# V and the projection strips in two halves of the tokens, every strip group by seven block products

## The chip, the cores and the metric

The kernel runs on one core of a Trainium2 chip. The metric is device time in microseconds of one execution, here the median of several runs.

## The reference, cut to what matters

Float32 inputs: x is 2048 x 1024, the combined projection `w_in` is 1024 x 5120.

```python
h = rms_norm(x, norm_g)
proj = einsum('bsd,de->bse', h, w_in)          # 2048 x 1024 by 1024 x 5120
u_pool, z_pool, q, k, v, z_attn, gate_logits = split(proj)
y_pool = multiscale_pool(u_pool, pool_w, pool_scale) * silu(z_pool)
attn = stick_breaking_attention(q, k, v)       # causal, 8 heads of 64
y_attn = attn * silu(z_attn)
gates = sigmoid(gate_logits + b_gate)
merged = gates[0] * (y_pool @ w_pool_up) + gates[1] * (y_attn @ w_attn_up)
x = x + merged @ w_out
return rms_norm(x, final_g)
```

`multiscale_pool` takes, for four groups of 128 channels of u, the trailing mean over 2, 4, 8 and 16 positions minus the value itself, then a 128 x 128 map and a scale per channel.

## The kernel before, in words

**Three matmuls for one.** Every float32 operand of a product is split into a high part (a copy to the type fp32r, by ScalarE) and a low part (the difference, by VectorE or GpSimd). `split3` (L73) makes one product of three matmuls: high by high, high by low, low by high. A product of 128 x 128 weights with 512 tokens is the unit; a strip is 128 columns of `w_in`, and one strip for one chunk of 512 tokens is 8 k-tiles, so 24 matmuls (`strip_product`, L85).

**Seven block products.** Two strips by two chunks of tokens, cut in halves of k, are a product of 2 x 2 blocks. By a Winograd scheme it takes seven block products (parts) of 4 k-tiles, 12 matmuls each, instead of eight. It needs forms of the weights (S1 to S4, four 128x512 operations) and of h (T1 to T4), and the parts' results are added up in sums (`take`, `add_part`, `join`). Names: A11, A12, A22, S1 to S4 are weight operands; B11, B21, B22, T1 to T4 are their partners made of h. The sizes of blocks: a form of h in `hT` has 4 k-tiles by 512 tokens, high and low.

**The four stages**, each a block of programs for all engines with a barrier behind it:

- `stage1` (L307): for each of 16 tiles of 128 tokens, the RMS statistics (ScalarE squares, VectorE `mean` L486, `factors` L493 with the diagonal at L504), TensorE spreads the factor over partitions (`spread`, L539), VectorE scales the transposed x (`scale` L472, at L481, 8 operations), ScalarE makes the high part (L435), GpSimd the low part (L401), and TensorE makes V for the tile, 24 matmuls (L551, L559, L567). VectorE copies V out (L470). TensorE goes through the tiles in the order of the tokens. V's weights (`wv_hi`, `wv_lo`) are split once. At its end TensorE makes the first plain unit of the first strip.
- `stage2` (L610): 12 strips (u in four groups, then the eight of q and k) and part of the z_pool strips, all by plain units: 49 units of 24 matmuls, in the order of the list `units`. High parts of a strip's weights by ScalarE (L794), low ones by GpSimd (L887). The four groups of u go through the pooling on VectorE (L999 levels, L1009, the cast L1016, L1018) over all 2048 tokens, and TensorE maps the result (`mix`, L1045). Late in this stage VectorE makes T1 to T4 from high and low parts of h (`first_forms` L947, `last_forms` L964), for tokens of both halves: those of chunks 2 and 3 go to the scratch `form_scratch` in HBM, those of chunks 0 and 1 in place at the end (L983). For the last strips and z_pool it runs through the chunks in the order 2, 3, 0, 1.
- `stage3` (L1111): attention for four pairs of heads, 320 items, and between them a filler of the rest of the strips (z_pool, z_attn, gates). The filler is a generator (`projections`, L1526) that the item loop advances by a table: each item has a cost, and `due` (L1208) says how many filler matmuls are done after it. Group 0 is four plain parts, of which one is made in stage 2; groups 1 to 23 are seven parts each. All other engines follow the same table (`PART_END`, `W_STEP`, `RESULT`). Weights of a part go through a ring of five slots: ScalarE's high (L1600), then GpSimd's low (`step` in `low_w`, L1770), as soon as the part five before is done.
- `stage4` (L1867): the gated merge, the output projection (by seven parts too) and the last norm.

**Order.** Every engine runs its program in order and waits on semaphores. All loads and stores are issued by SyncE (SP) in one queue. GpSimd's operations in stage 3 each wait for the one before.

## Time and profile before

| what | value |
|---|---|
| median of 3 runs | 1587.72 us (1587.53 to 1587.85) |
| span of the profiled execution | 1586.6 us |
| TensorE matmuls | 1556.0 us busy, 98% of the span, 7926 |
| VectorE | 1236.3 us, 78% |
| ScalarE | 772.7 us, 49% |
| GpSimd | 1004.9 us, 63% |
| mean granted clock of TensorE | 0.997 |
| DMA | 245.79 MB, mean 155 GB/s |

The profile is one execution, taken by the hardware profiler; its own time is known as its span, from the first to the last instruction, and the median of the runs is 1.1 us above it. PE is TensorE, PEld its weight loads, DVE VectorE, ACT ScalarE, POOL GpSimd, SP SyncE. Busy time of PE is the union of matmuls that overlap in the array, so the duration of one matmul is more than the distance to the next.

### The profile page before, as it was taken

The numbers are of one execution on the slowest core, as the hardware profiler recorded it, in microseconds if no ns is written. First come the engines' busy times: TensorE is split into PE (matmuls) and PEld (weight loads), VectorE is DVE, ScalarE is ACT, GpSimd is POOL, SyncE is SP. The second block draws the span as 40 slices with busy tenths as digits, with TensorE's granted clock in tenths as the row PEclk, the third lists the DMA queues.
The fourth block names the chain that finished last, engine by engine and source line by source line (L and its number), as shares of the span: only waits on it lengthen the run. The fifth ranks groups of instructions, "written<-read, shape, count | busy, mean of one in ns | idle before, by whom it ended". The sixth has DMA issues, their size and how long they took to land. (4 is left out here: it accounts for less than half of the span.)

```text
span 1586.6 us, 24736 instructions
## 1 busy us (share of the span) xinstructions
PE 1556.0 (98%) x7926; PEld 1299.3 (82%) x7926; DVE 1236.3 (78%) x1658; ACT 772.7 (49%) x1490; POOL 1004.9 (63%) x707
## 2 busy tenths in 40 slices
PE   7999999999999999999998999999999999999998
PEld 6888888888888888888877888888788788888886
DVE  6745424784888889998898988889888756677987
ACT  4422222214666666666665666666666512233342
POOL 4531102431788888888877887889986534456774
PEclk9999999999999999999999999999999999999999
DMA  7633335665434243343595443333422687864552
GB/s 246 231 129 145 133 108 184 241 182 161 128 116 113 79 119 104 108 136 91 174 317 182 121 129 87 111 106 110 119 78 65 206 280 252 262 196 161 184 189 110
DMA packets 164225, 245.79 MB, mean 155 GB/s; under 512 B 47729, under 2 KB 81009, under 8 KB 164098
## 3 DMA queue, kind: packets, MB, share of 16 engines
q1 hardware_dynamic: 164098, 244.20, 49.4%
q8 instruction: 67, 1.10, 0.3%
q14 instruction: 60, 0.49, 0.1%
HBM read 158.15 MB, written 85.99 MB: 154 GB/s over the span
## 5 line engine op out<-in xcount | busy, mean ns | idle before, releaser
L1697 DVE TENSOR_TENSOR_SCAN left<-keep,left 128x512 f32<-128x512 f32 x192 | 301.6, 1571 | 39.9 <-issue 23.4
L1770 POOL TENSOR_TENSOR ring<-raw,ring 128x512 fp32r<-128x512 f32 x138 | 240.1, 1740 | 71.8 <-ACT ring L1600 56.6
L1517 PE MATMUL psum<-hT,ring 128*128 128x512 f32 x644 | 264.1, 410 | 4.9 <-DMA hT<-form_scratch 3.6
L1521 PE MATMUL psum<-hT,ring 128*128 128x512 f32 x644 | 262.5, 408 | 0.0
L1519 PE MATMUL psum<-hT,ring 128*128 128x512 f32 x644 | 261.8, 407 | 0.0
L1606 ACT ACTIVATE keep<-psum 128x512 f32<-128x512 f32 (+3 forms) x320 | 170.9, 534 | 139.8 <-PE psum L1543 131.6
L1613 ACT ACTIVATE wt<-psum 128x512 fp32r<-128x512 f32 (+3 forms) x320 | 170.8, 534 | 104.8 <-PE psum L1551 102.0
L1703 DVE TENSOR_TENSOR wt<-psum,wt 128x512 fp32r<-128x512 f32 (+3 forms) x320 | 189.6, 593 | 11.6 <-ACT wt L1613 8.5
L1563 PEld LDWEIGHTS psum<-wt,vm 128*128 128x128 f32 x1088 | 170.9, 188 | 26.6 <-issue 1.5
L1563 PE MATMUL psum<-wt,vm 128*128 128x256 f32 x1088 | 181.3, 281 | 0.4 <-DVE row_sum L1712 0.4
L1551 PE MATMUL psum<-ident,left 128*128 128x128 f32 x1088 | 170.9, 272 | 2.5 <-DVE wt L1703 2.3
L1551 PEld LDWEIGHTS psum<-ident,left 128*128 128x128 f32 x1088 | 136.2, 140 | 44.5 <-issue 6.6
L1694 DVE TENSOR_TENSOR_SCAN left<-keep,floor 128x512 f32<-128x512 f32 (+3 forms) x128 | 143.6, 1122 | 20.2 <-ACT keep L1606 18.2
L75 PE MATMUL psum<-hT,w_parts 128*128 128x512 f32 x392 | 152.6, 389 | 0.5 <-POOLq L899 0.5
L77 PE MATMUL psum<-hT,w_parts 128*128 128x512 f32 x392 | 152.5, 389 | 0.0
L76 PE MATMUL psum<-hT,w_parts 128*128 128x512 f32 x392 | 152.5, 389 | 0.0
L1517 PEld LDWEIGHTS psum<-hT,ring 128*128 128x128 f32 x644 | 121.6, 189 | 26.5 <-issue 4.2
L1521 PEld LDWEIGHTS psum<-hT,ring 128*128 128x128 f32 x644 | 121.6, 189 | 17.9
L1519 PEld LDWEIGHTS psum<-hT,ring 128*128 128x128 f32 x644 | 121.6, 189 | 17.1
L887 POOL TENSOR_TENSOR w_parts<-w_raw,w_parts 128x1024 fp32r<-128x1024 f32 x13 | 34.5, 2654 | 149.0 <-ACT w_parts L794 149.0
L1770 POOL TENSOR_TENSOR y_out<-row_sum 64x128 f32<-64x128 f32 x128 | 110.5, 863 | 26.0 <-DVE row_sum L1712 8.5
L1542 PE MATMUL psum<-km,qm 128*128 128x512 f32 (+3 forms) x320 | 115.9, 362 | 3.6 <-DMA qm<-qk_scratch 1.8
(232 smaller groups left out, 3338.7 us busy)
## 6 DMA issues: line engine op xcount, KB each, us to landing
raw<-in_w_strips SPq DMA_DIRECT2D x92, 256.0 KB, 4.0
qm<-qk_scratch SPq DMA_DIRECT2D x128, 128.0 KB, 4.1
gate<-gate_scratch SPq DMA_DIRECT2D x64, 256.0 KB, 4.5
hT<-form_scratch SPq DMA_DIRECT2D x28, 512.0 KB, 8.6
xt<-in_x SPq DMA_DIRECT2D x16, 512.0 KB, 5.0
xT<-in_x_T SPq DMA_DIRECT2D x16, 512.0 KB, 3.9
qk_scratch<-staging SPq DMA_DIRECT2D x32, 256.0 KB, 2.8
qk_scratch<-store_lo SPq DMA_DIRECT2D x32, 256.0 KB, 3.5
```

The lines of the kernel that those rows point to most:

```text
L75: pe.matmul(out, w_hi, m_hi, start=start, stop=False)
L76: pe.matmul(out, w_hi, m_lo, start=False, stop=False)
L1517: pe.matmul(o, hi, m_hi, start=k == 0, stop=False)
L1519: pe.matmul(o, hi, m_lo, start=False, stop=False)
L1521: last = pe.matmul(o, lo, m_hi, start=False, stop=k == HK - 1)
L1551: last = pe.transpose(bank_t(n)[:, j * P:(j + 1) * P], left[:, n % LN, a:a + P], ident[:, :])
L1563: last = pe.matmul(bank_o(row), vm[:, t % VN, j, :], wt[:, n % WN, j, :, :].rearrange("p a q -> p (a q)"), start=first and j == 0, stop=fi ...
L1606: act.activation(keep[:, n % 2, CH - w:CH], bank_s(n)[:, 0:w], ACT.Sigmoid, scale=-SCALE).then_inc(keep_done, 1)
L1613: act.activation(wt[:, n % WN, 0:w // P, 0, :], bank_t(n)[:, 0:w].rearrange("p (j q) -> p j q", q=P), ACT.Copy).then_inc(wt_hi_done, 1)
L1697: dve.tensor_tensor_scan(left[:, n % LN, span][:, ::-1], k, k, carry, ALU.mult, ALU.bypass).then_inc(scanned, 1)
L1703: dve.tensor_tensor(wt[:, n % WN, 0:w // P, 1, :], bank_t(n)[:, 0:w].rearrange("p (j q) -> p j q", q=P), wt[:, n % WN, 0:w // P, 0, :].bit ...
L1770: pool.tensor_tensor(out_, a, b, op).then_inc(s, 1)
```

## The change

`stage1` and `stage2` are replaced by one block, `front`. The tokens are taken in two halves of 1024. For each half it makes V for eight tiles and then six groups of seven parts (two of u, four of q and k); a slot of its schedule is one V tile or one part. The order is 8 tiles, 42 parts, 8 tiles, 42 parts, 2 parts of stage 3's group 0.

- Tiles of a half alternate between its two chunks, so that after every second tile T1 to T4 can be made for 128 columns. They are made during V, from the scaled fp32 tiles (`xT`, scaled in place) as far as these are there: six VectorE operations per pair of tiles (`first_forms`, `last_form`), four high parts on ScalarE (`form_high`), and low parts on VectorE (`form_lows`) but for those in `LATE_T`, which GpSimd makes (T3 in the first half, T3 and T4 in the second).
- The copy of V out of PSUM moves from VectorE to ScalarE and has one buffer. The statistics of tiles 8 to 15 are made between parts of the first half (`STAT_PARTS`). V's weights are loaded and split a second time (`RELOAD`), since the pooling uses their place.
- The strips' weights go through the ring of five in the front too, and each strip is loaded once per half. A strip group has five additions (`add_part`) and two joins on VectorE, two copies of PSUM (`take`) on ScalarE; for q and k also four high copies (`result_high`) on ScalarE and four low parts (`result_low`) on VectorE.
- Pooling works on 1024 tokens at a time, in steps between the parts, with the last 16 columns kept (`tail`); the four mixes of a half come after its parts 12, 16, 20 and 24.
- All seven forms of the first half are stored to the scratch during the first 28 parts. Stage 3 then begins with the second half of the tokens.
- In stage 3 group 0 is made of seven parts like the others; the first two of them are made in the front. The filler goes from 2004 matmuls to 1992.

The diff, cut to its core:

```diff
-def strip_product(pe, out, w_hi, w_lo, hT, c):
...
-        stage1(nc, sem, psum, Arena(nc, free_at, end), ident, ident_r, gcol, bcol, pscol,
...
-        stage2(nc, sem, psum, Arena(nc, free_at, end), Arena(nc, free_at, heads.at), Arena(nc, heads.at, end), ident, v_d,
...
+        front(nc, sem, psum, at, free_at, hT_at, ident, ident_r, gcol, bcol, pscol, v_ends, hT, ring, raws, staging,
+              x, x_T, norm_gT, w_v, b_gateT, pool_scaleT, w_strips, pool_w, pool_fix, v_d, qk_d, mix_d, form_d, head_loads)
...
+FRONT_GROUPS, FRONT_TILES = 12, TT // 2
+HALF_GROUPS = FRONT_GROUPS // 2
+HALF_PARTS = HALF_GROUPS * FORMS
+READY_PARTS = 2
+def tile_slot(n):
+    return n if n < FRONT_TILES else n + HALF_PARTS
+def part_slot(r):
+    return r + FRONT_TILES if r < HALF_PARTS else r + 2 * FRONT_TILES
...
+    LATE_T = {0: (T3,), 1: (T3, T4)}
+    T_ORDER = (T3, T1, T2, T4)
...
+    MIX_AFTER = (12, 16, 20, 24)
+    STAT_PARTS = {n: 14 + 2 * (n - FRONT_TILES) for n in range(FRONT_TILES, TT)}
+    RELOAD = 28
```

On GpSimd:

```diff
+            def tile_step(n):
+                tile_low(n)
+                if n % FRONT_TILES >= 2:
+                    if n % 2 == 0:
+                        form_low(n - 1, T3)
+                    elif T4 in LATE_T[n // FRONT_TILES]:
+                        form_low(n - 2, T4)
...
+            for s in range(SLOTS):
+                n = step_at(s)
+                if n is not None:
+                    tile_step(n)
...
+                if s == 5:
+                    pool.wait_ge(pw_hi_done, 1)
+                    step(pw_lo[:, :, :], pw[:, :, :], pw_hi[:, :, :].bitcast(F32), ALU.subtract, pw_lo_done, 1)
+                for w in splits_at(s):
+                    low_w(w)
```

On VectorE:

```diff
+            def first_forms(n):
...
+                dve.tensor_tensor(raw_t(n, T3), scaled(n, 1), scaled(n, 0), ALU.subtract).then_inc(t_raw, 1)
+                dve.tensor_tensor(raw_t(n, T1), scaled(n, 0), tile_of(n - 1, 0, 0).bitcast(F32),
+                                  ALU.subtract).then_inc(t_raw, 1)
+                dve.wait_ge(t_raw, RAW_OPS * pair + 2)
+                dve.tensor_tensor(raw_t(n, T1), raw_t(n, T1), tile_of(n - 1, 0, 1).bitcast(F32),
+                                  ALU.subtract).then_inc(t_raw, 1)
+                dve.wait_ge(t_raw, RAW_OPS * pair + RAW_OF[T1])
+                dve.tensor_tensor(raw_t(n, T2), scaled(n, 1), raw_t(n, T1), ALU.subtract).then_inc(t_raw, 1)
...
+            def tile_step(n):
+                i = n % FRONT_TILES
+                first = n < FRONT_TILES
+                if first and i + 1 < FRONT_TILES:
+                    mean(n + 1)
+                scale(n)
+                if i + 1 < FRONT_TILES:
+                    if first:
+                        factors(n + 1)
+                    make_diag(n + 1)
+                if i % 2 == 1:
+                    if i >= 3:
+                        form_lows(n - 2)
+                    first_forms(n)
+                elif i >= 2:
+                    last_form(n - 1)
```

On TensorE:

```diff
+            def make_part(r):
+                g, j = divmod(r, FORMS)
+                if r >= 4:
+                    g0, j0 = divmod(r - 4, FORMS)
+                    if j0 in (A11, S1):
+                        pe.wait_ge(taken, 2 * g0 + (1 if j0 == A11 else 2))
+                    else:
+                        pe.wait_ge(summed, 5 * g0 + ADD_OF[j0])
+                pe.wait_ge(w_lo_done, r + 1)
...
+            for s in range(2, SLOTS):
+                if s in TILE_AT:
+                    project_v(TILE_AT[s])
+                else:
+                    r = PART_AT[s]
+                    make_part(r)
```

`closing_at` gives, in the slot of the last tile of a half, the forms that are left: VectorE's `last_form` and `form_lows`, GpSimd's T3 (and T4). `splits_at` gives ring low 0 in slot 5, 1 and 2 in slot 6, 3 and 4 in slot 7, and then ring low r + 5 in the slot after part r. `low_w` has, for a group's first operand, S3 and S2 ahead of the ring low and S1 behind it, and S4 behind the second's.

## Rows read from the trace of the kernel before

**Rows 1.** Busy time by stretch: count in brackets, then granted clock, DMA share, GB/s.

```profile
0.00:109.00 109.00, 101.06 (x438) 81.52 (x439) 70.06 (x226) 46.84 (x87) 51.16 (x43) 0.98 0.64 215
109.00:389.00 280.00, 279.20 (x1229) 229.44 (x1228) 149.12 (x155) 71.57 (x113) 67.36 (x47) 1.00 0.50 164
```

**Rows 2.** TensorE's waits from 0 to 410 us, the longest in total.

```profile
PE psum L539 <- DVE spare L504: 2.9, 3, 1.3
```

**Rows 3.** TensorE's timeline at the boundary of stages 1 and 2: start, duration.

```profile
109.04 0.39 PE L75 MATMUL psum<-hT,w_parts 128*128 128x512 f32 x1
...
114.26 0.39 PE L77 MATMUL psum<-hT,w_parts 128*128 128x512 f32 x1
115.16 0.47 PE L75 MATMUL psum<-hT,w_parts 128*128 128x512 f32 x1 [0.51 <-POOLq L899]
```

**Rows 4.** TensorE's timeline in the V stage, two spreads in a row.

```profile
64.52 0.38 PE L539 MATMUL psum<-spare 128*128 128x128 f32 x2
...
70.23 0.38 PE L539 MATMUL psum<-spare 128*128 128x128 f32 x2
```

**Rows 5.** VectorE's timeline in the V stage, tile 2 and a later one.

```profile
24.04 2.16 DVE L481 SCALAR_TENSOR_TENSOR scaled<-xT,gcol,psum 128x128 f32<-128x128 f32 x8 [1.32 <-PE psum L539]
...
65.00 2.16 DVE L481 SCALAR_TENSOR_TENSOR scaled<-xT,gcol,psum 128x128 f32<-128x128 f32 x8 [1.21 <-PE psum L539]
67.07 0.68 DVE L470 COPY staging<-psum 128x512 f32<-128x512 f32 x1
67.67 0.14 DVE L488 TENSOR_SCALAR stat<-stat 128x1 f32<-128x1 f32 x1
...
68.28 0.27 DVE L496 TENSOR_SCALAR stat<-stat 128x1 f32<-128x1 f32 x1 [0.27 <-ACT stat L424]
...
68.78 0.71 DVE L504 TENSOR_SCALAR spare<-ident,stat 128x128 f32<-128x128 f32 x1
```

**Rows 6.** Timeline of the same tile, ScalarE's first high part and GpSimd's two low parts.

```profile
66.15 0.63 ACT L435 ACTIVATE hT<-scaled 128x512 fp32r<-128x512 f32 x1 [2.39 <-DVE scaled L481]
...
66.86 2.54 POOL L401 TENSOR_TENSOR hT<-scaled,hT 128x512 fp32r<-128x512 f32 x2 [0.80 <-ACT hT L435]
```

**Rows 7.** Timeline of forms of h in the strip stage, VectorE and GpSimd.

```profile
299.87 0.68 DVE L956 TENSOR_TENSOR t_raw<-hT 128x512 f32<-128x512 f32 x1
300.47 0.68 DVE L958 TENSOR_TENSOR t_raw<-hT 128x512 f32<-128x512 f32 x1
...
306.36 0.69 DVE L975 TENSOR_TENSOR t_raw<-hT,t_raw 128x512 f32<-128x512 f32 x1
...
307.07 1.28 POOL L893 TENSOR_TENSOR t_parts<-t_raw,t_parts 128x512 fp32r<-128x512 f32 x1 [2.02 <-ACT t_parts L831]
...
307.08 1.81 DVE L977 TENSOR_TENSOR t_raw<-t_raw,hT 128x512 f32<-128x512 f32 x1
```

**Rows 8.** Timeline in stage 4, two VectorE operations on SBUF and one of GpSimd.

```profile
1407.53 2.39 DVE L2359 TENSOR_TENSOR form_t<-late,form_t 128x512 fp32r<-128x512 f32 x2
...
1407.69 1.67 POOL L2511 TENSOR_TENSOR rows<-rows,gate 128x512 f32<-128x512 f32 x1 [3.87 <-DVE gate L2331]
```

**Rows 9.** Groups of VectorE, 109 to 389 us, pooling: busy us, mean ns.

```profile
L999 DVE TENSOR_TENSOR sums<-u 128x2048 f32<-128x2048 f32 x4 | 9.2, 2293 | 53.3 <-ACT u L809 53.3
...
L1016 DVE CAST pl_hi<-pooled 128x2048 fp32r<-128x2048 f32 x4 | 4.9, 1224 | 0.1
```

**Rows 10.** GpSimd's ring lows (ns, min/median/max), and the busy time of stage 4's parts.

```profile
L1770 POOL TENSOR_TENSOR ring<-raw,ring x138: 1274/1757/3603, 409.1 to 1229.8; 128x512 fp32r<-128x512 f32 x138
...
1459.00:1478.00 19.00, 19.00 (x84) 15.63 (x85) 17.26 (x30) 6.91 (x15) 12.57 (x8) 1.00 0.54 193
```

**Rows 11.** Busy time around tile 2, granted clock third from the end, and TensorE's timeline there.

```profile
24.00:28.00 4.00, 2.95 (x12) 1.80 (x10) 3.58 (x14) 2.17 (x4) 2.09 (x2) 1.00 0.32 96
28.00:32.00 4.00, 3.49 (x10) 2.84 (x10) 3.12 (x10) 1.39 (x4) 1.17 (x2) 0.58 0.99 341
...
28.94 2.05 PE L559 MATMUL psum<-wv_lo,hT 128*128 128x512 f32 x4
```

**Rows 12.** SP's timeline in the strip stage, four form stores.

```profile
160.50 3.60 SPq L728 DMA_DIRECT2D form_scratch<-hT  x4
```

More of the change, by code:

```diff
@@ new lines, in make_diag, with scale @@
+            def make_diag(n):
+                dve.wait_ge(statistics, 4 * n + 4)
+                if n >= 2:
+                    dve.wait_ge(spread_done, n - 1)
+                dve.tensor_scalar(diag[:, n % 2, :], ident[:, :], stat[:, n, 3:4], stat[:, n, 5:6],
+                                  ALU.mult, ALU.mult).then_inc(diag_done, 1)
+            def scale(n):
+                dve.wait_ge(xT_in[n % 3], DMA * (n // 3 + 1))
+                dve.wait_ge(spread_done, n + 1)
+                for k in range(KT):
+                    tile = xT[:, n % 3, k, :]
+                    last = dve.scalar_tensor_tensor(tile, tile, gcol[:, k:k + 1], spread_bank(n), ALU.mult, ALU.mult)
+                    if k % HK == HK - 1:
+                        last.then_inc(scaled_done, 1)
@@ L531, in _ @@
+            assert nexts == [None, None]
         @block.tensor
         def _(pe):
-            def spread(t):
-                pe.wait_ge(diag_done, t + 1)
-                if t >= 2:
-                    pe.wait_ge(scaled_done, 2 * (t - 1))
-                pe.matmul(psum[:, t % 2, 0:P], ones[:, :], diag[:, t % 2, :], start=True,
-                          stop=True).then_inc(spread_done, 1)
-            def part_of(t, k, part):
-                return tile_of(t, k // HK, part)[:, k % HK, :]
@@ L545, in high_high, with spread, part_of @@
-            def high_high(t, ks):
+            def spread(n):
+                pe.wait_ge(diag_done, n + 1)
+                if n >= 2:
+                    pe.wait_ge(scaled_done, 2 * (n - 1))
+                pe.matmul(spread_bank(n), ones[:, :], diag[:, n % 2, :], start=True, stop=True).then_inc(spread_done, 1)
+            def part_of(n, k, part):
+                return tile_of(n, k // HK, part)[:, k % HK, :]
+            def high_high(n, ks):
+                f, i = divmod(n, FRONT_TILES)
@@ new lines, in mix @@
+            def mix(f, q):
+                win = POOL_ORDER[q]
+                pe.wait_ge(pool_lo, 4 * f + q + 1)
+                if f == 0 and q == 0:
+                    pe.wait_ge(pw_lo_done, 1)
+                for c in range(2):
+                    tok = slice(c * CH, (c + 1) * CH)
+                    if q == 0:
+                        pe.wait_ge(v_copied, FRONT_TILES * (f + 1))
+                    else:
+                        pe.wait_ge(mix_out, mix_use(f, q - 1, c) + 1)
+                    split3(pe, v_bank(c), pw_hi[:, win, :], pw_lo[:, win, :], pl_hi[:, tok], pl_lo[:, tok],
+                           True, True).then_inc(mixed, 1)
@@ L1843, in _ @@
             for s in range(-9, END):
-                for g in range(1, GROUPS):
+                for g in range(GROUPS):
                     for j in (S1, S3):
```

1519 lines of the change are left out of this document (774 added, 745 removed).

## The prediction

> **What bounds the kernel now.** I read the busy time by stage first: in the V stage (0 to 109 us) TensorE is busy 101 of 109 us, in the strip stage (109 to 389) 279.2 of 280 [rows 1]. TensorE's own waits come next: the largest sum in the first 410 us is 2.9 us, for the diagonal that `spread` reads [rows 2]. So the front is TensorE issuing matmuls at its own pace. A strip product's matmuls start 5.22 us apart over 23 steps, 0.227 us each [rows 3]; the 389 ns "mean of one" overlaps the next matmul and would overstate a matmul by 1.7 times. A V tile's cycle is 5.71 us, from one `spread` to the next [rows 4].
>
> **What is removed.** Before: 49 plain strip units of 24 matmuls in the strip stage and its first unit in stage 1, plus 3 plain parts in stage 3; of these 48 units belong to the twelve u, q, k strips and 4 to z_p's first group. Thirteen groups of four units (96 matmuls) become seven parts of 12 (84). That is 13 x 12 = 156 matmuls fewer; V (384), the mixes (48) and stage 4 keep theirs. 156 x 0.227 = **-35.4 us**, all on the path. One stage boundary goes: the next matmul after 114.26 came at 115.16 instead of 114.49 [rows 3], -0.7. Together -36.1, if TensorE stays the bound.
>
> **What VectorE gets in V.** Now a tile costs VectorE: scale 2.07 us (from 65.00 to 67.07), means 0.33, factors 0.50, diag 0.28, taken as free of GpSimd [rows 5]; the V copy moves to ScalarE. New per pair of tiles in the first half: six tensor_tensor to make T1 to T4 and three low parts, all with two SBUF operands. Such operations start 0.60 us apart, 0.72 when one waits for the one before [rows 7]. Per pair: 2 x 3.18 + 9 x 0.60 + 3 x 0.13 = 12.2 us, against 2 x 5.71 = 11.42 for TensorE. Already over.
>
> Worse is GpSimd. A VectorE operation on two SBUF tiles that is issued at 307.08 beside a GpSimd one (307.07, 1.28 us) takes 1.81 instead of 0.68: it starts when the other has ended [rows 7]. And of two such VectorE operations in a row with GpSimd waiting, GpSimd gets in between: 1.67 us instead of 1.28, and the two take 2.39 [rows 8]. So they take turns: 1.28 held by GpSimd, 0.54 by VectorE. The diag does so too: 0.71 us at 68.78, ending just as GpSimd's low parts do (66.86 + 2.54) [rows 5, 6].
>
> Laid along one tile with the scale's start at 0: ScalarE's first high part 1.15 [rows 5, 6], GpSimd's lows 1.86 to 3.14 and 3.25 to 4.5, with diag between them; VectorE's next form waits until 4.5. An odd tile then has three lows and four forms: 1 + 6 more at 0.60, gaps 0.4, mean 0.33, period 9.4. An even one has two forms with GpSimd's T3 low between them: 4.5, 5.1, 6.4, 6.9, mean, period 7.3. A pair is 16.7 us, not 11.42.
>
> First half: VectorE is free at 22.7 before scale(2), which starts at 24.0 [rows 5]; four forms of tile 1 (2.4 + 0.4) and a mean (0.33) put it at 25.8. Scale(7) comes 7.3 + 9.4 + 7.3 + 9.4 + 7.3 = 40.7 later, at 66.5, and V(7) starts 1.8 after it, at 68.3. Now V ends at 109.0 [rows 3], so V(7) starts at 57.6 and ends at 109.0 - 8 x 5.71 = 63.3. Before `tile_low(7)` GpSimd's order has pw_lo, S3, S2, the first ring low and S1: five operations, 6.4 us, with VectorE's lows and T3 in turn another 2; so V(7)'s low operand is there at 76, and V(7) ends near 79.5, 16.2 later than now. T2's low part is behind a closing sequence of VectorE and GpSimd in turn, 2.6 us late for part 2. Sum **+19**. Bounds: 3, if VectorE never waits (12.2 a pair); 25, if it waits in full for all five GpSimd operations of each of three pairs (12.2 + 6.4 = 18.6).
>
> Second half: statistics are made earlier, three low operations become two, and GpSimd has T3 and T4. The same laying out gives 9.6 and 7.0; from scale(9) (8.3, no lows yet, but a ring low) to scale(15) 8.3 + 7.0 + 9.6 + 7.0 + 9.6 + 7.0 = 48.5. Scale(9) starts 1.5 after V(8), so V(15) ends 1.5 + 48.5 + 1.8 + 5.5 = 57.3 after V(8) starts, not 8 x 5.71 - 0.15 = 45.5, and T2's low is 1.7 late: **+13.5**; bounds 0 (VectorE alone: 2 x 2.35 + 8 x 0.60 + 0.4 = 9.9 a pair, under 11.42) and 18 (9.9 + 6 x 1.28 = 17.6 a pair).
>
> **The strips.** A group is 84 x 0.227 = 19.05 us of TensorE, 114.3 for a half's six, and mixes add 24 x 0.227 = 5.4. GpSimd has 7 ring lows and 4 forms a group, 11 x 1.28 = 14.1 (its unhindered minimum, 1.27 [rows 10]), no joins. VectorE holds the shared turn for 2 joins and, for q and k, 4 lows: 3.3. Together 17.4 of 19.05. Stage 4 does the same seven parts with 8 GpSimd operations, 7 lows and two 128x1024 finishes, 10.2 + 3.8 + 2.1 = 16.1, and TensorE is busy 19.00 of 19.00 us there [rows 10]. So a q or k group is covered. Pooling isn't: per half ten levels, four pooled and four pl_lo at half of 2.29 less overhead, 1.08, and four casts at 0.55, about 22 us [rows 9], in parts 6 to 21. There the turns want 25 x 1.28 + 22.4 + 5 = 59.6 us where TensorE offers 16 x 2.72 + 4.1 = 47.6. That is 12 us late, taken up partly by the ring (five splits ahead) and the four banks. With the ring just filled and GpSimd late in the first half: **+8**; second half, ring full: **+5**. Bounds 0 (all absorbed) and 13 each. The second loading of V's weights (2 MB), its four lows (1.2 each [rows 9], in the lock sum 4.3) and 6 MB more of strips lie beside parts; before, DMA ran at half share there [rows 1], cost nothing if it lands some parts early, which parts 28 to 40 give it.
>
> **The clock.** With V bound by VectorE, TensorE idles some 2.6 of 8.3 us. From 24 to 28 it was busy 2.95 of 4 us, and from 28 to 32 the granted clock was 0.58, a stretch at 1.2 GHz between stretches at 2.4; the four matmuls from 28.94 took 2.05 instead of 1.07 [rows 11]. That drop cost about 1.6 us (eight matmuls in 3.4 us, not 1.8). In most tiles such a drop fits in the idle time; the ends of V(7) and V(15) don't have it. **+3**, bounds 0 and 13 x 1.6 = 21.
>
> The Trainium skill (TensorE: Matmul & The Clock Gate, "Why this matters for your kernels") puts a fall of the clock down to an idle gap between bursts of matmuls, a whole one, not to a partly busy stretch. By that rule this term would be 0 and the sum 1597; the rows show the fall after a stretch 74% busy. The same page (Back-to-back issue gap) gives 131 ns a matmul of 512 columns in a real stream; by it 156 matmuls would be an estimated 20.4 us, and the sum 1615. The trace has 227.
>
> **Sum.** -36.1 + 19 + 13.5 + 8 + 5 + 3 = +12.4 on the profiled span of 1586.6. The median of the runs shown is 1587.7, 1.1 above that span; I add it: **1600 us**.
>
> Edits at nothing: SP issues per strip group 4 loads, up to 8 stores of results and 7 of forms; at the 0.90 us of a form store, the longest here [rows 12], 19 issues take 17 of 19.05 us, and the first wait in its order is for results of two parts before, so nobody waits for it while it keeps up; the 80 VectorE operations that make the forms in the strip stage now hide under TensorE, and their removal gives nothing; V's stores share one buffer, but have a tile's 5.7 us or more each; the key, query and value loads before stage 3 still have some twelve parts (33 us); stage 3 starts with group 0 as parts, and there TensorE's filler is spread over 1187 - 389 us as before.
>
> **Rivals.** (a) *TensorE bounds everything*: 1587.7 - 36.1 = 1551.6. For it: copies and statistics were moved off VectorE; against it, 12.2 us already exceeds 11.42 with no contention. 0.08. (b) *The other side: only V pays.* The turns shared by GpSimd and VectorE bind in V, but in the strips the ring and banks absorb pooling, and the clock holds: V costs 24 to 32, so 1587.7 - 36.1 + 28 = 1580. It decides at a total loss of 36: below, the change is faster. Against it: 59.6 us of turns in 47.6. 0.26. (c) *My forecast*, 1600, its own range 1588 to 1609: 0.46. (d) *The turns bind the strips through and through*: ScalarE's result copy waits for VectorE's sum and stands ahead of the next split, so a late VectorE makes GpSimd late with no slack to use; 13 in each half, and V's tiles at the half clock add 6 more: 1600 + 13 + 6 = 1619. 0.20.
>
> **The numbers.** 1600; the range takes in (b) and most of (d): 1564 to 1620; (a) and the tail of (d) stay out. A measurement of this kernel can tell 0.2%, 3.2 us. Faster: (a), (b) but its upper edge, a sliver of (c): 0.35. Same: edges of (b) and (c): 0.08. Slower: 0.57.
>
> **What would show it.** Right: in the new V stages TensorE's starts of tiles lie 7 to 9.5 us apart, alternating; its waits name ScalarE's or GpSimd's parts of h, VectorE is busy over 90%; form operations of 1.8 us beside GpSimd ones; TensorE waits for ring lows in parts 8 to 24 and hardly later; the granted clock in V is under 0.9. Wrong: V tiles at 5.7 us; no wait of TensorE on the ring; GpSimd operations at 1.3 throughout; a matmul spacing other than 0.227; or a wait on the reload of V's weights, the one transfer that I cost at nothing.

## The result and the profile after

| what | before | after |
|---|---|---|
| median of 4 runs each | 1587.62 us | 1657.62 us (1654.57 to 1660.69) |
| ratio | | 1.0443, 95% interval 1.0422 to 1.0464 |
| span of the profiled execution | 1586.6 us | 1658.9 us |
| TensorE matmuls | 1556.0 us busy, 7926 | 1552.7 us busy, 7770 |
| VectorE | 1236.3 us | 1354.2 us |
| GpSimd | 1004.9 us | 1188.5 us |
| mean granted clock | 0.997 | 0.979 |

The change is 70 us slower, where 12 were forecast and 1620 was the upper end. The 156 matmuls are gone; all of the loss is waiting and half clock. First the busy time by stretch, cut at the starts of the first matmul of V, of the first strips, of the second V, of the second strips, and at the end of the front; columns as in [rows 1] (busy us of PE, PEld, DVE, ACT and POOL, each with its count).

```profile
0.00:79.60 79.60, 61.52 (x230) 46.89 (x231) 64.16 (x139) 38.70 (x71) 45.95 (x37) 0.91 0.52 182
79.60:227.20 147.60, 127.59 (x532) 101.19 (x530) 108.84 (x139) 58.34 (x108) 104.09 (x66) 0.95 0.80 261
227.20:290.70 63.50, 52.62 (x206) 41.69 (x207) 58.33 (x98) 22.58 (x40) 41.44 (x28) 0.89 0.28 89
290.70:431.90 141.20, 130.80 (x557) 106.53 (x555) 102.16 (x98) 45.11 (x80) 105.45 (x67) 0.96 0.49 135
```

Where [rows 1] had TensorE busy 279.2 of 280 us in the strips, it now has 127.6 of 147.6 and 130.8 of 141.2. The granted clock is under 1 in every stretch. TensorE's waits from 0 to 450 us (total, times, longest), against 2.9 us in [rows 2]:

```profile
PE psum L1167 <- ACT staging L797: 19.5, 6, 4.7
PE psum L75 <- ACT staging L848: 15.7, 3, 6.4
PE psum L1655 <- ACT sum_a L1767: 7.0, 1, 7.0
PE psum L75 <- DVE staging L1016: 5.0, 1, 5.0
PE psum L75 <- POOL ring L680: 3.3, 3, 1.7
```

The two largest name ScalarE, the least busy engine: its copy of V (L797) and its scale of a mix (L848), both into the one buffer `v_out`. Neither is slow itself (0.6 us); each stands behind other work. The first, at tile 2 of V, from the timelines of DVE, ACT, PE:

```profile
29.89 1.64 DVE L964 TENSOR_TENSOR raw_forms<-raw_forms,hT 128x512 f32<-128x512 f32 x1
33.56 2.16 DVE L935 SCALAR_TENSOR_TENSOR xT<-xT,gcol,psum 128x128 f32<-128x128 f32 x8 [1.24 <-PE psum L1155]
28.24 0.63 ACT L787 ACTIVATE hT<-xT 128x512 fp32r<-128x512 f32 x1 [0.41 <-DVE xT L935]
28.77 1.65 ACT L791 ACTIVATE hT<-raw_forms 128x512 fp32r<-128x512 f32 x3
30.33 0.58 ACT L797 ACTIVATE staging<-psum 128x512 f32<-128x512 f32 x1
30.96 2.07 PE L1167 MATMUL psum<-wv_hi,hT 128*128 128x512 f32 x4 [4.71 <-ACT staging L797]
```

V(0) has long been done, but its copy comes after tile 2's high parts and three of the forms. TensorE starts 4.71 us late and at the half clock (four matmuls in 2.07 us), its `spread` comes late, and VectorE waits 1.24 us for that: the lateness goes round. A mix's scale, from the timelines around mix 2 of the first half:

```profile
144.88 2.15 DVE L1056 TENSOR_TENSOR level<-u 128x1024 f32<-128x1024 f32 x1
148.05 0.69 DVE L1026 TENSOR_TENSOR front_sum_c<-front_sum_d,front_sum_c 128x512 f32<-128x512 f32 x1
148.77 0.63 ACT L831 ACTIVATE front_store<-front_sum_c 128x512 fp32r<-128x512 f32 x1 [5.14 <-DVE front_sum_c L1026]
149.83 0.67 ACT L848 ACTIVATE staging<-psum,pscol 128x512 f32<-128x512 f32 x1
150.55 0.79 PE L75 MATMUL psum<-pl_hi,pw_hi 128*128 128x512 f32 x1 [6.40 <-ACT staging L848]
```

Pooling holds VectorE, the join comes late, ScalarE's result copy waits 5.14 us for it, the scale of the mix before stands behind that copy, and TensorE waits 6.40 us with its parts behind the mix. Before part 79 it is a transfer:

```profile
398.21 2.40 SPq L564 DMA_DIRECT2D raw<-in_w_strips  x4
408.33 0.43 DVE L123 TENSOR_TENSOR v_raw<-v_prev,v_raw 128x256 f32<-128x256 f32 x1 [10.40 <-DMA v_prev<-v_scratch]
409.46 0.68 DVE L1016 TENSOR_TENSOR staging<-psum,staging 128x512 f32<-128x512 f32 x1
410.20 0.80 PE L75 MATMUL psum<-hT,ring 128*128 128x512 f32 x1 [4.97 <-DVE staging L1016]
```

The value load was issued behind four loads of strips, VectorE waited 10.40 us for it, and additions queued behind. And in the closing of the first V the turns are as forecast:

```profile
72.71 1.53 POOL L680 TENSOR_TENSOR b<-xT,b 128x512 fp32r<-128x512 f32 x1
74.39 1.54 POOL L680 TENSOR_TENSOR hT<-xT,hT 128x512 fp32r<-128x512 f32 x1
73.04 1.75 DVE L947 TENSOR_TENSOR raw_forms<-xT,hT 128x512 f32<-128x512 f32 x1
74.82 1.66 DVE L950 TENSOR_TENSOR raw_forms<-raw_forms,hT 128x512 f32<-128x512 f32 x1
```

**Stage 3.** Its first filler matmul starts 7.4 us after the last of the front (the wait L1655 above). The last store of the front is issued at 434.3, and SyncE issues the next block's first load at 438.4: the front ends only when its last results have landed. The boundary before took 0.84 us. Then its items themselves are slower: from the first score to the last 863.1 us, 847.2 before. One place, 30 us after the start:

```profile
465.69 1.53 POOL L1901 TENSOR_TENSOR sum_c<-sum_d,sum_c 128x512 f32<-128x512 f32 x1
467.26 0.63 ACT L1781 ACTIVATE staging<-sum_c 128x512 f32<-128x512 f32 x1 [3.85 <-POOL sum_c L1901]
467.92 1.26 DVE L1868 TENSOR_TENSOR sum_c<-sum_c,staging 128x512 f32<-128x512 f32 x1 [1.82 <-ACT staging L1781]
469.10 0.68 DVE L1834 TENSOR_TENSOR wt<-psum,wt 128x512 fp32r<-128x512 f32 x1
469.93 0.62 PE L1686 MATMUL psum<-ident,left 128*128 128x128 f32 x3 [3.36 <-DVE wt L1834]
```

**Where the 72.3 us of the span come from.** The front, had TensorE bounded it, would have brought stage 3's first matmul from 389.6 to 356 us (144 matmuls and one boundary less); it came at 439.1. The 83 between are: first V +16, first strips +28 (147.6 against 42 x 12 + 24 matmuls at 0.227, which are 119.8), second V +18 (63.5 against 8 x 5.71), second strips +16 (140.9 against 44 x 12 + 24 matmuls, 125.3), the end of the front +7, and -2 since the old strip stage was not quite at 0.227 either. After it: 12 matmuls fewer -2.7, items and their start some +20, the rest (last score to last matmul) +5. With the 33.5 that the front saved, 83 - 33.5 - 2.7 + 20 + 5 = 72.

### The profile page after: what moved, and what is told of

It reads as the page before. It is cut to its first block and busy times, and to the rows that moved or that the text cites. A ratio compares the mean times of both kernels' runs of the same rounds, so it can differ in the third digit from the quotient of the medians.

```text
span 1658.9 us, 25189 instructions
## 1 busy us (share of the span) xinstructions
PE 1552.7 (94%) x7770; PEld 1285.2 (77%) x7770; DVE 1354.2 (82%) x1753; ACT 824.9 (50%) x1597; POOL 1188.5 (72%) x818
## 5 line engine op out<-in xcount | busy, mean ns | idle before, releaser
L1901 POOL TENSOR_TENSOR ring<-raw,ring 128x512 fp32r<-128x512 f32 x140 | 236.7, 1690 | 80.9 <-ACT ring L1735 65.7
L1655 PE MATMUL psum<-hT,ring 128*128 128x512 f32 x664 | 273.3, 412 | 12.2 <-ACT sum_a L1767 7.0
L1659 PE MATMUL psum<-hT,ring 128*128 128x512 f32 x664 | 271.2, 408 | 0.0
L1657 PE MATMUL psum<-hT,ring 128*128 128x512 f32 x664 | 270.8, 408 | 0.0
L1834 DVE TENSOR_TENSOR wt<-psum,wt 128x512 fp32r<-128x512 f32 (+3 forms) x320 | 189.5, 592 | 12.4 <-ACT wt L1748 9.5
L1686 PE MATMUL psum<-ident,left 128*128 128x128 f32 x1088 | 171.3, 272 | 11.3 <-DVE wt L1834 11.1
L680 POOL TENSOR_TENSOR ring<-raw,ring 128x512 fp32r<-128x512 f32 x76 | 119.9, 1578 | 72.0 <-ACT ring L841 64.3
L1825 DVE TENSOR_TENSOR_SCAN left<-keep,floor 128x512 f32<-128x512 f32 (+3 forms) x128 | 139.2, 1088 | 20.1 <-ACT keep L1741 18.1
L1655 PEld LDWEIGHTS psum<-hT,ring 128*128 128x128 f32 x664 | 126.0, 190 | 34.3 <-ACT sum_a L1767 7.8
L75 PE MATMUL psum<-hT,ring 128*128 128x512 f32 x344 | 137.6, 400 | 11.9 <-DVE staging L1016 5.0
L1659 PEld LDWEIGHTS psum<-hT,ring 128*128 128x128 f32 x664 | 126.0, 190 | 18.5
L1657 PEld LDWEIGHTS psum<-hT,ring 128*128 128x128 f32 x664 | 126.2, 190 | 17.5
L76 PE MATMUL psum<-hT,ring 128*128 128x512 f32 x344 | 136.2, 396 | 0.0
L77 PE MATMUL psum<-hT,ring 128*128 128x512 f32 x344 | 136.1, 396 | 0.0
```

The lines of the kernel that those rows point to most:

```text
L75: pe.matmul(out, w_hi, m_hi, start=start, stop=False)
L76: pe.matmul(out, w_hi, m_lo, start=False, stop=False)
L77: return pe.matmul(out, w_lo, m_hi, start=False, stop=stop)
L1655: pe.matmul(o, hi, m_hi, start=k == 0, stop=False)
L1657: pe.matmul(o, hi, m_lo, start=False, stop=False)
L1659: last = pe.matmul(o, lo, m_hi, start=False, stop=k == HK - 1)
```

## The experiments

The table has the medians, the ratio to the kernel before on the same chip, and, from each one's trace, the start of V(7)'s last matmul and the lengths (starts of first matmuls) of first strips, second V, second strips, the way from the front's last matmul to stage 3's first, and the items (first score to last).

| run | us | ratio (95%) | V(7) | strips 1 | V 2 | strips 2 | gap | items |
|---|---|---|---|---|---|---|---|---|
| changed | 1657.6 | 1.0443 (1.0422-1.0464) | 79.4 | 147.6 | 63.5 | 140.9 | 7.4 | 863.1 |
| e1 copy first | 1651.8 | 1.0404 (1.0384-1.0423) | 79.5 | 148.8 | 56.0 | 138.4 | 7.8 | 862.8 |
| e2 statistics late | 1656.8 | 1.0437 (1.0416-1.0458) | 77.7 | 147.5 | 61.3 | 141.4 | 8.4 | 864.7 |
| e3 values | 1661.0 | 1.0470 (1.0444-1.0496) | 79.9 | 147.6 | 61.3 | 135.1 | 11.4 | 861.7 |
| e4 no forms | 1643.6 | 1.0349 (1.0328-1.0370) | 75.9 | 147.7 | 51.5 | 139.9 | 8.1 | 863.7 |
| e5 low 7 first | 1656.0 | 1.0413 (1.0384-1.0443) | 71.7 | 155.4 | 57.7 | 140.2 | 8.5 | 865.1 |
| e6 pooling small | 1645.6 | 1.0358 (1.0341-1.0374) | 76.9 | 140.7 | 61.2 | 131.0 | 9.1 | 867.6 |
| e7 small stores | 1649.3 | 1.0394 (1.0373-1.0416) | 79.1 | 145.6 | 62.6 | 138.1 | 7.4 | 857.9 |
| e8 GpSimd small | 1630.4 | 1.0268 (1.0253-1.0283) | 76.0 | 139.1 | 59.2 | 130.8 | 6.3 | 861.2 |
| e9 phase | 1646.7 | 1.0364 (1.0337-1.0390) | 77.7 | 151.6 | 60.7 | 140.7 | 8.2 | 852.5 |
| e10 orders | 1627.1 | 1.0234 (1.0207-1.0260) | 79.6 | 141.9 | 55.9 | 132.1 | 8.6 | 853.7 |
| e11 bare | 1599.2 | 1.0062 (1.0038-1.0086) | 67.7 | 134.7 | 46.0 | 131.6 | 4.4 | 857.3 |
| e12 bare and orders | 1568.4 | 0.9876 (0.9844-0.9908) | 67.2 | 124.9 | 47.9 | 125.6 | 3.2 | 844.6 |
| e13 warm | 1658.6 | 1.0440 (1.0403-1.0476) | 77.9 | 147.8 | 60.2 | 139.6 | 8.1 | 862.1 |

The columns are of one profiled execution each, the medians of all runs. Where kernels have the same code, a column shows how far two executions lie apart: V(7) 76.9 to 79.9 and the second V 60.7 to 63.5 (changed, e2, e3, e6, e7, e9), first strips 147.6 to 151.6 (changed, e3, e9), items 861.2 to 867.6 (changed, e1 to e6, e8, e13). Differences below 4 us in one column, 7 in that of the items, show nothing by themselves.

### e1: ScalarE's copy of V first

```diff
             def tile_step(n):
...
+                if n % FRONT_TILES >= 2:
+                    copy_v(n - 2)
                 tile_high(n)
...
-                    copy_v(n - 2)
```

> ScalarE's copy of V out of PSUM is moved in its own order: ahead of the tile's high parts and of the forms' high parts, instead of behind them. Theory 1 (order: TensorE waits in V for a copy that stands behind other work on ScalarE, six times, 19.5 us in all, and VectorE then waits for a late spread): the six waits named after the copy go, even tiles start 2 to 3 us earlier, the clock holds there, and the kernel gets 10 to 20 us shorter than the changed one (1638 to 1648). Theory 2 (the prediction's: VectorE and GpSimd take turns and bind the V tiles): the waits only change their name, to VectorE's scale, and the time stays within 4 us of 1657.6.

1651.8 us, 5.8 less: between the two. The waits for the copy are gone; TensorE's largest in V are now these:

```profile
PE psum L1168 <- ACT hT L787: 8.5, 4, 2.6
PE psum L1187 <- POOL b L680: 6.4, 1, 6.4
```

The second V is 7.5 us shorter (63.5 to 56.0), the first ends where it did, since V(7) now starts earlier and waits 6.4 us for GpSimd's low part instead. So the order cost about 6 us in the second V: of the 19.5 us of waits that named ScalarE's copy, 5.8 came back. VectorE and GpSimd hold the rest.

### e2: statistics' loads later

```diff
-                        if r == first - 4:
+                        if r == first - 1:
                             load_xt(m)
```

> The loads for the statistics of tiles 8 to 15 are issued three parts later in SyncE's order, where the wait for the tile before (a square on ScalarE) is already met. Theory 1 (order: SyncE waits there for ScalarE's square, ScalarE waits for the stores that stand behind it on SyncE, and the scale of a mix stands behind those): the waits of the mixes 2 and 3 in the first half (6.4 and 4.6 us) shrink below 1.5 us each, the two falls of the clock behind them go, and the kernel is 8 to 14 us shorter (1643 to 1650). Theory 2 (pooling on VectorE is late because of the turns): the waits stay, within 3 us of 1657.6.

1656.8 us, first strips 147.5: no effect. The longest wait for a mix's scale is still 5.9 us. That theory of the mixes fell; their chain goes through VectorE (above), not through the stores.

### e3: value tiles

```diff
-    V_PARTS = [HALF_PARTS + i for i in (29, 31, 33, 35)]
+    V_PARTS = [HALF_PARTS + i for i in (26, 30, 34, 38)]
...
-                    if r == first + 1:
+                    if r == first + 2:
                         head_loads.value_diff(dve, u)
```

> The first four value tiles for the attention are loaded at parts 26, 30, 34, 38 of the second half instead of 29, 31, 33, 35, and VectorE works on each one part later after its load than before. Theory 1 (VectorE waits up to 10.4 us for such a load, issued behind four loads of strips, with TensorE's additions behind it): the wait of 5.0 us before part 79 goes with the half clock behind it, 5 to 8 us shorter (1650 to 1653). Theory 2 (turns): TensorE waits there for another addition or ring low instead, within 3 us of 1657.6.

1661.0 us. The wait before part 79 went, and the second strips are 5.8 us shorter; the gap behind the front grew from 7.4 to 11.4 us, and the median is no better. What was gained was paid at the next wait, the end of the block. (The profiled execution took 1655.3 us, 5.7 under the median of its runs.)

### e4: no forms in V

```diff
-                dve.tensor_tensor(raw_t(n, T3), scaled(n, 1), scaled(n, 0), ALU.subtract).then_inc(t_raw, 1)
+                dve.tensor_tensor(raw_t(n, T3)[:, :, 0:4], some, some, ALU.add).then_inc(t_raw, 1)
...
+                act.activation(low_t(n, j), source, ACT.Copy)
+                act.activation(high_t(n, j), source, ACT.Copy).then_inc(t_hi, 1)
```

> As the first of these four, and the making of T1 to T4 in V is left out (VectorE's and GpSimd's operations for them shrink to 4 of 128 columns, ScalarE writes copies of an h tile in their place, one activation more each): the sums of the front are not those of the reference. Theory 2 (turns bind V): V's tiles go at 5.7 to 6.3 us, V(7) ends near 65 and the second V takes 47 us, 25 to 33 us less than the changed kernel, nearly all of it beyond what the first of these runs gives. Theory 1 (order alone): the first run has already given most of it, and this one is less than 8 us under it.

14.0 us under the changed kernel, 8.2 under e1. (All forms and their lows are cut like the first line shown.) The second V falls to 51.5 (45.7 at TensorE's pace); the first gains 3.6 at most, for it still waits for GpSimd's ring work ahead of tile 7's low parts. Beyond e1 the forms are worth 3.6 and 4.5 us in the two V, at the edge of what a column tells: a part of V's price, not most of it. The 8.2 us under e1 are just over the bound of theory 1 and far from what theory 2 asked.

### e5: tile 7's low parts ahead of the ring

```diff
-            return {5: (0,), 6: (1, 2), 7: (3, 4)}.get(s, ())
+            return {6: (0, 1), 7: (2, 3, 4)}.get(s, ())
...
-                if s == 5:
+                if s == 6:
                     pool.wait_ge(pw_hi_done, 1)
```

(with e1's edit)

> As the run with ScalarE's copy of V first, and GpSimd's (and ScalarE's) work on pool_w and on the first three slots' strip weights is moved one slot back, behind the low parts of tile 7. The theory that V(7) waits 6.4 us for GpSimd's order alone: V(7) ends near 75 instead of 79.5, and the kernel takes 4 to 5 us less than that run (1647). Rival: the same five operations then hold the ring's first lows or T3's low for parts 0 to 2, and the time comes out within 2 us of that run.

V(7) ends at 71.7, 7.8 us sooner than in e1, and the first strips take 155.4 instead of 148.8; 1656.0 us, 4.2 above e1, and the intervals of the two ratios overlap. The first part now waits 3.3 us for a ring low of GpSimd's, one of the five operations, and part 2 3.7 us for a form's low part of VectorE's; between 0 and 200 us these are

```profile
PE psum L75 <- POOL ring L680: 3.9, 2, 3.3
PE psum L75 <- DVE hT L974: 3.7, 1, 3.7
```

The strips end no sooner than in e1 (230.9 against 228.5 us): V's end and the strips' start are one budget of GpSimd and VectorE, and this order within it gives nothing.

### e6: most of the pooling left out

```diff
-                        dve.tensor_tensor(to[:, a:W], src[:, a:W], src[:, a - (1 << i):W - (1 << i)],
+                        dve.tensor_tensor(to[:, a:PAD + 64], src[:, a:PAD + 64], src[:, a - (1 << i):PAD + 64 - (1 << i)],
```

> The changed kernel with the pooling left out but for 32 to 80 of its 1024 columns (levels and pooled; its high and low parts are copies of u, the low one a single-operand copy), so the mix scratch is not the reference's. Theory A (pooling makes VectorE late, with GpSimd in turn, and everything behind it: ScalarE's result copies, the scale of a mix, the ring): the strips of the first half take 126 to 132 us instead of 147.6, those of the second 128 to 132 instead of 141, some 25 us less in all (1632). Theory B (the DMA engines, at a share of 0.84 to 1.05 from 143 to 227 us, land results and form stores late): the first half loses only what lies before 143 us, 3 to 8 us, and the kernel 5 to 12.

12.0 us less: 7 in the first strips, 10 in the second; the items, whose code is the same, took 4.5 more in this execution. Half of what theory A asked, and at the upper end of theory B's, which e7 takes up; the first strips are still 21 us above 119.8.

### e7: a quarter of the form stores

```diff
-                sp.dma_start(form_d[j, kk], hT[:, HOME[j], kk, :, :].bitcast(F32)).then_inc(form_stored, DMA)
+                sp.dma_start(form_d[j, kk][:, :, 0:P], hT[:, HOME[j], kk, :, 0:P].bitcast(F32)).then_inc(form_stored, DMA)
```

> The changed kernel with a quarter of each form stored and loaded back (128 of 512 columns, 28 transfers of 128 KB instead of 512 KB each way), so stage 3's second half works on other numbers. Theory B (DMA): the waits after 143 us in the first half (mix 3's 4.6 us, ring lows of parts 31 to 37, the end) go, 8 to 14 us less (1645 to 1650). Theory A (VectorE and GpSimd): within 3 us of 1657.6, since the waits come through additions and ring lows that wait for no transfer.

(The load back is cut in the same way.) 8.3 us less, as theory B had it, but not where it had it: the first strips lose 2 us only, within the scatter, and 5.2 us lie in the items, where the forms are loaded back, 3.3 below the lowest of the same code. Where the rest of the 8.3 lies is open. The DMA engines, busy at a share of 0.80 in the first strips, are not what holds them.

### e8: GpSimd's strip work left out

```diff
-                step(ring[:, w % RING, 1, :, :], at_g[j][:, :, :], ring[:, w % RING, 0, :, :].bitcast(F32),
+                step(ring[:, w % RING, 1, :, 0:4], at_g[j][:, :, 0:4], ring[:, w % RING, 0, :, 0:4].bitcast(F32),
...
+                act.activation(ring[:, w % RING, 1, :, :], source, ACT.Copy)
```

> The changed kernel with GpSimd's work on strip weights in the front left out: S1 to S4 and the low parts on 4 of 128 columns, and ScalarE writes high and low slot as copies of one block (one activation more per part), so V is right and the strips are not. Theory A: without turns VectorE's operations in the strips take 0.6 to 0.7 and 1.2 us instead of 1.3 to 1.8 and 2.2, pooling comes in time, and the strips take 122 to 130 us in the first half and 126 to 132 in the second, 25 to 35 us less in all (1623 to 1633). Theory B: the late stores stay, less than 10 us.

(S1 to S4 are cut in the same way.) 27.2 us less, the most of any single edit; of the 32.0 between the two profiled executions 8.5 are in the first strips, 10 in the second, 3.4 and 4.3 in the two V, where GpSimd's strip work at V's end is left out too. VectorE's operations on the pooled columns, of e8 (count, ns min/median/max), and then of the changed kernel:

```profile
L1079 DVE CAST pl_hi<-level x4: 684/686/710, 101.9 to 144.5; 128x1024 fp32r<-128x1024 f32 x4
L1083 DVE TENSOR_TENSOR pl_lo<-level,pl_hi x4: 1224/1225/1225, 102.6 to 145.2; 128x1024 fp32r<-128x1024 f32 x4
```

```profile
L1076 DVE CAST pl_hi<-level x4: 680/1174/1785, 109.4 to 156.2; 128x1024 fp32r<-128x1024 f32 x4
L1080 DVE TENSOR_TENSOR pl_lo<-level,pl_hi x4: 1226/2194/2200, 110.6 to 157.0; 128x1024 fp32r<-128x1024 f32 x4
```

The same operations, without GpSimd beside them, take 0.69 and 1.23 us at every time, and up to 1.79 and 2.20 with it. This shows the turns directly, for the cast too, which has a single operand. The Trainium skill ("SBUF — State Buffer", Terms) says that the port pair which the two engines share is held for a full instruction and the loser blocks; the rows agree.

### e9: the phase of stage 3's filler

```diff
-        n = round(run / sum(cost) * (TOTAL - KEPT))
+        n = round(run / sum(cost) * (TOTAL + PART - KEPT)) - PART
```

> The changed kernel with one line of stage 3's filler table changed, so that every part from group 1 on ends at the same item as in the kernel before (now most end one or two items earlier, since group 0 has 60 matmuls left instead of 72). Phase theory: attention's 320 items took 863 us instead of 847 in steps of 6, 3, 3.5 and 2.6 us in the first 130 items, because parts now meet VectorE and GpSimd work of the items at another place; with the old places they take 845 to 851, the kernel 12 to 17 us less (1641 to 1646). Group theory: only group 0, whose joins on GpSimd hold ScalarE's result and VectorE behind it at 465 to 469 us, costs anything, and the later steps stay: 4 to 6 us less (1652 to 1654) or nothing.

11.0 us less, and the items 852.5 us instead of 863.1. Against the kernel before, the items ran 5.9 us behind after 16 of them, 8.3 after 48, 11.3 after 96, 14.9 after 128; now 4.3, 3.9, 4.2 and 4.2. In the trace every part from group 1 on now ends at the same item as in the kernel before. So two thirds of stage 3's loss was the phase: the later steps are gone, and the first stays. That it comes from group 0 made as parts is argued (the rows at 465 us), since no run has it plain.

### e10: all changes of order together

The edits of e1, e2, e3 and e9, and

```diff
+                for f, q in mixes_at(s - 1):
+                    scale_mix(f, q, 0)
+                for f, q in mixes_at(s - 3):
+                    scale_mix(f, q, 1)
                 r = PART_AT.get(s - 1)
...
-                sp.wait_ge(out_lo, m + 1)
+                sp.wait_ge(out_hi, m + 1)
                 sp.dma_start(qk_d[0, i, :, tok], store[:, m % 2, :].bitcast(F32)).then_inc(hi_stored[m % 2], DMA)
+                sp.wait_ge(out_lo, m + 1)
```

> All changes of order together, nothing left out: ScalarE's copy of V first, its scale of a mix ahead of the slot's results, statistics' loads three parts later, value loads earlier with VectorE's work a part later, the store of a result's high part issued before the wait for its low part, and the filler table as in the run with its phase. If order is what costs in the strips: first half 147.6 to under 138, second 141 to under 132, and with the phase 1657.6 to 1615 to 1630. If the strips are held by VectorE and GpSimd themselves: the strips stay within 3 us each, and only V's 6 us and the phase's gain show (1636 to 1648).

1627.1 us with nothing left out, 30.5 less: V 2 and the items as in e1 and e9, the strips 5.7 and 8.8. Of TensorE's waits up to 440 us these are the largest:

```profile
PE psum L1657 <- ACT sum_a L1769: 8.3, 1, 8.3
PE psum L75 <- POOL ring L681: 6.7, 6, 1.8
```

The mixes' scale, 15.7 us before, is below these with 2.4, and GpSimd's ring lows are next in the strips. This is the best whole version found, and still 2.3% above the kernel before.

### e11 and e12: everything left out

e11 has the edits of e1, e4, e6, e7 and e8, e12 those and all of e10.

> ScalarE's copy of V first, and all four suspects left out at once: the making of T1 to T4 in V, GpSimd's work on strip weights, most of the pooling, three quarters of the form stores (the sums of the front are not the reference's). Alone these gave 14, 27, 12 and 8 us; if they add up, 61 us: 1597, front ended near 371 us. If they stand in for one another (each wait taken away uncovers the next), the sum is 35 to 50: 1608 to 1622. If something else holds the strips (ScalarE's order, SyncE, the banks), the strips still take over 132 us in a half.

> Everything left out as in the bare run, and all changes of order with the phase of the filler table. If the list of causes is complete, TensorE now bounds the front: strips of the first half 120 to 126 us, of the second 126 to 130 (with 45.5 to 47 for the second V), items 852 us, and the time is 1599.2 less about 10 (strips of the first half), 2 (second), 5 (phase): 1580 to 1585, so that the 156 matmuls saved show at last, under the kernel before. If a cause is missing, the strips stay at 132 and more and the time over 1590.

e11 took 1599.2, 58.4 us less, near the 61 of the four alone: the causes add up. But its strips still took over 131 us. TensorE's waits for a mix's scale up to 450 us, of e6 (pooling out) and then of e11 (all four out):

```profile
PE psum L75 <- ACT staging L848: 8.1, 2, 6.7
```

```profile
PE psum L75 <- ACT staging L855: 6.4, 2, 4.1
```

Of 15.7 us some 6 to 8 stay with the pooling out: what is left goes only with the orders (2.4 in e10, none in e12). With the orders it is 1568.4, under the expected 1580: less than the kernel before by 1.2% (interval 0.9 to 1.6). Busy time of e12 by the same stretches:

```profile
0.00:67.40 67.40, 55.98 (x230) 42.52 (x231) 43.05 (x141) 47.66 (x90) 32.13 (x38) 1.00 0.62 219
67.40:192.50 125.10, 121.12 (x532) 99.08 (x531) 58.07 (x136) 80.24 (x151) 17.13 (x67) 0.99 0.73 221
192.50:240.50 48.00, 48.00 (x208) 39.56 (x209) 37.73 (x99) 33.20 (x61) 23.62 (x26) 0.95 0.37 116
240.50:366.00 125.50, 125.50 (x556) 103.58 (x554) 51.91 (x96) 68.77 (x124) 16.84 (x67) 1.00 0.52 158
```

TensorE is busy 125.50 of 125.50 us in the second strips, where the matmuls alone give 125.3, and 48.00 of 48.00 in the second V (45.7 alone; the granted clock was 0.95). So the saving is real once nothing else binds, and the list of causes is complete to within the first V (4 us late), 2 us of the second and 5 us of the first strips. The orders are worth 9.8 and 6.0 us of the two strips in this kernel, 5.7 and 8.8 in the whole one (e10).

### e13: TensorE kept busy in V's waits

```diff
+                    if n % FRONT_TILES >= 2 and n % 2 == 0:
...
+                        keep_warm(pe, psum[:, 3, :], ident_r, 10)
                     project_v(n)
```

> The changed kernel with ten matmuls whose result nobody reads ahead of the tiles 2, 4, 6, 10, 12 and 14 of V (10 x 0.227 = 2.3 us, inside the waits of 2.2 to 4.7 us there). If the falls of the clock in V come from TensorE's idle time there and cost some 1.5 us each on the path, five or six of them go and the kernel takes 5 to 9 us less (1649 to 1653), with fewer matmuls at a distance of 0.43 us. If the tiles wait for VectorE's work anyway, so that a slow tile only ends in less idle time, the time stays within 2 us of 1657.6; if the added matmuls stand in the way, it is 2 to 6 us longer.

1658.6 us. Busy time from tile 2 to the end of the first V and over the second V, of e13 and then of the changed kernel:

```profile
24.00:77.90 53.90, 45.25 (x191) 35.67 (x190) 50.92 (x103) 26.10 (x50) 32.95 (x22) 0.97 0.42 143
225.90:286.00 60.10, 54.51 (x236) 43.61 (x237) 56.85 (x96) 21.97 (x39) 41.62 (x28) 0.97 0.30 94
```

```profile
24.00:80.00 56.00, 43.71 (x167) 34.19 (x166) 51.66 (x105) 26.08 (x50) 33.41 (x23) 0.88 0.40 140
227.00:291.00 64.00, 52.93 (x208) 41.97 (x209) 58.83 (x98) 22.67 (x41) 41.64 (x28) 0.89 0.28 89
```

The granted clock rises from 0.88 and 0.89 to 0.97 and 0.97, and the median does not move: in V a slow tile ends in less idle time, as the prediction had it for most tiles. This is shown for V only; in the strips and at stage 3's start it was not tried.

## Why the prediction was wrong

What held:
- **Removed.** Matmul spacing is 0.227 as before, the count fell by 156, and e12 shows the saving in the time: 1568.4, some 17 above rival (a)'s 1551.6, in a kernel that leaves work out and whose front and items are close to TensorE's pace.
- **V.** First half: V(7) was to end near 79.5 and T2's low to come 2.6 late, +19; its last matmul started at 79.4 and part 2 came 0.6 late, +17. The way there was in part luck: scale(7) started at 64.6 and not at 66.5, V(7) at 70.3 and not at 68.3, and what held was GpSimd's low part, there at 75.9 for the 76 forecast. Second: +13.5 against +18. GpSimd and VectorE alternate at 1.53 and 1.7 us. What the prediction missed is who holds TensorE: it named only their turns, but the copy of V stands behind the forms' high parts on ScalarE, which e1 prices at 6 us net, all of it in the second half. "V's stores share one buffer, but have a tile's 5.7 us or more each" looked at the stores and not at the copy's place in ScalarE's order.

What failed, largest first. On the span the miss is 60 us (1658.9 against 1599.0): first strips +20, second +11, the two V -3 and +4, the gap before stage 3 +7, its items and their start +20, the rest +5, less 3 for the clock and 2 for the old strips' pace (rounded).

- **"The strips": +8 and +5, measured +28 and +16.** The balance of turns over parts 6 to 21 (59.6 us wanted in 47.6) put the front 12 us late "taken up partly by the ring and the four banks". The direction was right: e6 and e8 take 17 and 19 us off both strips. The term was mis-sized by 31 us, and one step that it left out is shown: a late VectorE does not reach TensorE through ring and banks alone. It goes through ScalarE's result copy to the scale of a mix, to which the schedule gives one part's slack: 15.7 us in three waits, two in the first half. Of the first strips' 28 us, the work left out gives 13 (e11) and the orders 10 more (e12), and 5 stay open; in the whole kernel the orders give 6 (e10). Rival (d) had that chain but for the ring; it was given 0.20 and 13 us per half, and is the nearest of the four. Besides, GpSimd's operations take 1.5 to 1.6 us on average beside VectorE, where 1.28, "its unhindered minimum", was put in. How much that cost is open: part of it is the wait for VectorE's turn, which the sum has already, and GpSimd was idle for 43 of the 147.6 us. (The sum itself, 25 x 1.28 + 22.4 + 5, is 59.4.)
- **"Edits at nothing": stage 3 starts with group 0 as parts, and the filler is spread as before.** It cost about 16 us in the items, of which e9 gives back 10.6, and 7.4 at its start, where the stores of the last group must land before the block ends. The sum had no term for either. I had compared the number of filler matmuls and not the item at which each part ends: one or two items earlier than before for most parts of the first two thirds.
- **"The key, query and value loads ... still have some twelve parts (33 us)".** VectorE waits 10.4 us for a value load and TensorE 5.0 behind it. The room is in the schedule, but the load and VectorE's use of it are two slots apart, and the load, behind four others in SyncE's queue, landed 7.0 us after its issue. Taken away alone it gave nothing (e3): the end of the block took it.
- **The clock: +3, measured 18, partly hidden.** From the starts of matmuls, 101 lie 0.43 us apart instead of 0.227, against 11 before: 90 x 0.2 = 18 us. But for one group of two in V, each group of them begins within 3 us after a wait of 2.0 to 7.0 us. In V they cost little (e13). In the strips and at stage 3's start they stand behind a wait of 3 to 7 us on the path (as the 0.80 us of the matmul at 410.20), and are a part of the terms above, not a further one.
- **From the last score to the last matmul, +5**: no part of the prediction. The changed kernel and the thirteen others have 339.6 to 345.1 us there with the same code, before had 338.9. So up to 5 us is scatter, and whether some 3 us are real is open.

Of the signs named ahead: starts of V tiles 6 to 9.4 us apart (from tile 3 on), VectorE over 90% busy in V (51.7 of 56 us), forms of 1.7 to 1.8 us beside GpSimd's and a granted clock under 0.9 in V came true. "Its waits name ScalarE's or GpSimd's parts of h" did for 3.7 us of GpSimd's; the 19.5 of ScalarE's are its copy of V. Waits on ring lows "in parts 8 to 24 and hardly later" did not: they were in parts 31 to 37, small, and parts 8 to 24 had the mixes instead. The reload of V's weights held nobody for over 2 us.

Open: how the 5.7 and 8.8 us of e10 in the strips divide between the scale ahead of the results, the earlier store and, in the second, the value loads (5.8 alone in e3), since they ran together; and how far the half clock costs time in the strips.

## What to carry to other kernels

- When work is moved to a less busy engine, ask what stands ahead of it in that engine's order and who waits for it: TensorE's waits named the half idle ScalarE for 35 us here (19.5 and 15.7). What such waits are worth is less, since another often stands right behind: moving the copy gave 6 of the 19.5. A balance of busy time does not show that; a list of each engine's order by slot, with the wait that every entry has, does.
- A saving on the bounding engine is worth what its neighbours' slack allows. Here 36 us of matmuls were bought with work on the two engines that take turns. The kernel beats the old one only with that work left out and the orders changed (e12); with the work alone out it is 0.6% slower (e11), with the orders alone 2.3% (e10).
- Wherever a table spreads work over a loop, a small change of its total shifts the phase of all that follows: compare the step at which each piece ends, old and new.

## What was not expected of the hardware

- A VectorE cast with one SBUF operand waits for GpSimd as two-operand operations do: 1024 columns in 0.69 us alone, up to 1.79 beside GpSimd (the changed kernel's rows under e8). The Trainium skill ("VectorE: DVE Perf Modes", Two Vector instructions with no wait between them) describes a single-source operation in a two-port mode as reading through the interface shared with GpSimd; the rows fit that, and no run here tells the mode.
- The same code at the same place does not always take the same time: in three kernels whose code is equal up to there the first strips took 147.6, 147.6 and 151.6 us. Whether a kernel with many waits is also less repeatable as a whole is open: four runs of the changed kernel spread over 6.1 us (12.4 in e5), those of the kernel before over 1.2 in the four beside them, but over 4.5 to 8.3 in the sets of seven beside the experiments.
